# RWKV-7 scan on one core: the four chunk matrices of a tile of 96 tokens, whole 96x96 products against stacked 32x32 tiles

## What is computed

```python
# S_t = S_{t-1} diag(w_t) + (S_{t-1} a_t) b_t^T + v_t k_t^T ; y_t = S_t r_t
def step(s, inp):
    r_t, w_t, k_t, v_t, a_t, b_t = inp
    sa = jnp.einsum('bhvk,bhk->bhv', s, a_t)
    s = s * w_t[:, :, None, :] + sa[..., None] * b_t[:, :, None, :] \
        + v_t[..., None] * k_t[:, :, None, :]
    y_t = jnp.einsum('bhvk,bhk->bhv', s, r_t)
    return s, y_t
```

## Time and profile before

| | before |
|---|---|
| median of 3 runs | 2810.82 us (2810.22 to 2811.73) |
| profiled execution: its own time / its span | 2808.27 / 2806.5 us |
| PE, PEld, DVE, ACT busy | 94%, 92%, 64%, 42% of the span |
| granted TensorE clock, mean | 0.969 |
| scan loop | from about 1341 to 1854 us of the span |

### The profile page before, as it was taken

One profiled execution on the slowest core, in us unless ns is written; L12 is line 12 of the kernel. 1 busy time (PEld: TensorE's weight loads), 2 busy tenths in 40 slices (PEclk: granted clock), 3 DMA queues, 4 the chain that ended last, 5 costly groups with the idle time before them and its releaser, 6 DMA issues.

```text
span 2806.5 us, 54115 instructions
## 1 busy us (share of the span) xinstructions
PE 2639.1 (94%) x21933; PEld 2574.2 (92%) x21933; DVE 1782.8 (64%) x2235; ACT 1184.6 (42%) x1360; POOL 125.9 (4%) x121
## 2 busy tenths in 40 slices
PE   7999867999999999999899999989699999999996
PEld 7999857999999999999799999979699999999996
DVE  6675656666666666677656565556656666666666
ACT  4344523555444444456323222233444444444442
POOL 2000000100000000002000000000400000000003
PEclk9999978999999999999999999999799999999997
DMA  6555413565555556555232323334265555555552
GB/s 187 157 166 157 122 60 99 173 196 185 187 179 180 187 187 187 185 154 152 83 91 83 85 82 95 94 98 158 89 195 182 183 180 183 184 179 180 185 174 83
DMA packets 419321, 418.72 MB, mean 149 GB/s; under 512 B 15310, under 2 KB 417474, under 8 KB 418946
## 3 DMA queue, kind: packets, MB, share of 16 engines
q1 hardware_dynamic: 418722, 415.41, 48.2%
q10 hardware_dynamic: 496, 1.84, 0.2%
HBM read 415.10 MB, written 2.10 MB: 149 GB/s over the span
## 4 chain that ended last, share of the span: by engine, by line
PE 82%; DVE 10%; ACT 3%; PEld 2%; issue 1%; POOL 1%; DMA 0%; SPq 0%; ACTq 0%; DVEq 0%; POOLq 0%; PEldq 0%
PE psum L1887 25%; PE psum L1888 24%; PE psum L1889 24%; PE psum L2200 4%; DVE w_lo L998 3%; ACT w_hi L598 1%; DVE act_lo L1035 1%; DVE head_r L1109 1%; DVE mixed L1843 1%; PEld psum L1889 1%; PEld psum L1887 1%; PE psum L2356 1%; PEld psum L1888 1%; PE psum L2360 1%; PE psum L2251 1%
## 5 line engine op out<-in xcount | busy, mean ns | idle before, releaser
L1887 PE MATMUL psum<-act_hi,w_hi 128*128 128x256 f32 (+3 forms) x4880 | 1413.4, 290 | 54.2 <-DVE act_lo L1035 17.2
L1888 PE MATMUL psum<-act_lo,w_hi 128*128 128x256 f32 (+3 forms) x4880 | 1386.6, 284 | 0.0
L1889 PE MATMUL psum<-act_hi,w_lo 128*128 128x256 f32 (+3 forms) x4880 | 1383.0, 283 | 0.0
L598 ACT ACTIVATE w_hi<-raw 128x1024 fp32r<-128x1024 f32 x788 | 828.3, 1058 | 1138.0 <-PE psum L1889 1116.0
L998 DVE TENSOR_TENSOR w_lo<-raw,w_hi 128x1024 fp32r<-128x1024 f32 x788 | 958.2, 1229 | 503.2 <-ACT w_hi L598 502.3
L1887 PEld LDWEIGHTS psum<-act_hi,w_hi 128*128 128x128 f32 (+1 forms) x4880 | 928.4, 190 | 70.3 <-issue 28.9
L1888 PEld LDWEIGHTS psum<-act_lo,w_hi 128*128 128x128 f32 (+1 forms) x4880 | 929.2, 190 | 1.5 <-issue 0.7
L1889 PEld LDWEIGHTS psum<-act_hi,w_lo 128*128 128x128 f32 (+1 forms) x4880 | 928.8, 190 | 0.0
L1887 PE MATMUL psum<-ff_hi,w_hi 128*128 128x256 f32 x1280 | 363.7, 284 | 13.5 <-DVE up L1016 6.5
L1888 PE MATMUL psum<-ff_lo,w_hi 128*128 128x256 f32 x1280 | 361.4, 282 | 0.0
L1889 PE MATMUL psum<-ff_hi,w_lo 128*128 128x256 f32 x1280 | 361.2, 282 | 0.0
(11 more groups left out here) (338 smaller groups left out, 1811.5 us busy)
## 6 DMA issues: line engine op xcount, KB each, us to landing
raw<-in_w_in SPq DMA_DIRECT2D x188, 512.0 KB, 3.8
raw<-in_w_up SPq DMA_DIRECT2D x176, 512.0 KB, 3.6
raw<-in_w_down SPq DMA_DIRECT2D x176, 512.0 KB, 4.5
raw<-in_w_gate_up SPq DMA_DIRECT2D x176, 512.0 KB, 3.6
raw<-in_w_out SPq DMA_DIRECT2D x64, 512.0 KB, 4.5
x_rows<-in_x SPq DMA_DIRECT2D x2, 1024.0 KB, 6.2
out_x<-out_rows SPq DMA_DIRECT2D x8, 256.0 KB, 3.2
raw<-in_w_in SPq DMA_DIRECT2D x4, 384.0 KB, 3.4
```

Source lines behind the costliest of these rows:

```text
L598: act.activation(w_hi[:, slot], raw[:, slot], ACT.Copy).then_inc(S["hi_done"], 1)
L1887: pe.matmul(out_, wh, xh, start=first and r == 0, stop=False)
L1888: pe.matmul(out_, wh, xl, start=False, stop=False)
L1889: mm = pe.matmul(out_, wl, xh, start=False, stop=last and r == RK - 1)
```

## The change

Every product of the scan is cut to what is not known to be zero. Only the diagonal 32x32 chunk blocks of a score or power matrix are made; they stand stacked, chunk c on partitions 32c to 32c+31, 32 columns per head. So `ldt` to `p4` are [4, 32] instead of [4, 96] wide. Each product of a head becomes three, one per chunk, whose weights and results are at array position (32c, 32c); the scores are made at (64e, 32c), the parts of output and state at (32c, 64e) into three banks 5, 6, 7, one for each chunk, and the state steps at (64e, 64e) with a state of [128, 2, 64]. The masks are folded to 32 columns by POOL (11 more additions). The stages are merged into 12 slots with the same 336 rows; the last float32 stages before the steps are one stage, `um`. Some copies move between ACT and DVE. The zeroing of `mt` goes.

```diff
-            def each_head(lhs, rhs_, bank, wide=RB):
+            chunk = [slice(RC * c, RC * c + RC) for c in range(3)]
+            def each_tile(lhs, rhs_, bank, at, wide=RC):
                 for h in range(4):
-                    mm = pe.matmul(psum[0:RB, bank, wide * h:wide * h + wide], lhs[0:RB, h],
-                                   rhs_(h), start=True, stop=True)
+                    for s in chunk:
+                        mm = pe.matmul(psum[s, bank, at + wide * h:at + wide * h + wide],
+                                       lhs[s, h], rhs_(s, h), start=True, stop=True)
                 mm.then_inc(S["rw_tensor"], 1)
...
+                def scores(lhs, rhs, n, bank, at):
                     for p in range(2):
-                        for e in range(2):
-                            mm = pe.matmul(psum[0:RB, bank + e, 192 * p:192 * p + 192],
-                                           z_at(kind, e, p), a_and_r(e, p), start=True, stop=True)
+                        for c in range(3):
+                            for e in range(2):
+                                o = at + RC * n * p
+                                mm = pe.matmul(psum[chunk[c], bank + e, o:o + RC * n],
+                                               z_at(lhs, e, p, c), z_at(rhs, e, p, c, n),
+                                               start=True, stop=True)
...
+                scores(Z_B, Z_A, 2, 4, AT_LT)
+                scores(Z_A, Z_B, 1, 4, AT_L).then_inc(S["rw_tensor"], 1)
+                scores(Z_K, Z_A, 2, 6, 0).then_inc(S["rw_tensor"], 1)
                 fill()
                 pe.wait_ge(*rw_dve.at("rbt", it))
+                each_tile(M["ldt"], tile_of("ld"), 4, 0)
+                each_tile(M["ld"], tile_of("ldt"), 5, 0)
                 fill()
                 pe.wait_ge(*rw_dve.at("rkt", it))
...
+                pe.wait_ge(*rw_act.at("l2t_out", it))
+                pe.wait_ge(*rw_dve.at("l2_out", it))
+                each_tile(M["l2t"], tile_of("l2"), 5, 0)
+                each_tile(M["l2"], tile_of("l2t"), 4, 0)
+                each_tile(M["l2"], tile_of("p1"), 4, AT_P2)
                 fill()
                 pe.wait_ge(*rw_act.at("kv", it))
+                each_tile(M["akt"], lambda s, h: kv[s, 1, 64 * h:64 * h + 64], 7, 0, 64)
                 pe.wait_ge(*rw_act.at("l4_out", it))
                 pe.wait_ge(*rw_dve.at("p2", it))
+                each_tile(M["l4t"], tile_of("l4"), 5, 0)
+                each_tile(M["l4"], tile_of("p2"), 4, 0)
                 fill()
...
+                def by_head(lhs, rhs, at, wide, start=False, stop=False):
+                    for p in range(2):
+                        for c in range(3):
+                            for e in range(2):
+                                o = psum[halfp[e], STEP_BANK + c, at + wide * p:
+                                         at + wide * p + wide]
+                                mm = pe.matmul(o, lhs(chunk[c], 2 * p + e), rhs(chunk[c], 2 * p + e),
+                                               start=start and p == 0, stop=stop,
+                                               skip_group_check=True)
+                    return mm
+                by_head(u_part(0), tile_of("rbt"), AT_RU, RC, True, True)
+                by_head(u_part(0), b_part, AT_MT, 64, False, True)
+                by_head(u_part(1), tile_of("rbt"), AT_Y, RC)
+                by_head(tok(kv, 1), tile_of("rkt"), AT_Y, RC)
+                by_head(b_part, u_part(1), AT_ST, 64)
+                by_head(tok(kv, 0), tok(kv, 1), AT_ST, 64).then_inc(S["rw_tensor"], 1)
+                fill()
+                pe.wait_ge(*rw_dve.at("mt", it))
                 for c in range(3):
+                    pe.wait_ge(S["rw_s"], 10 * q + 1 + 3 * tt + c)
                     for p in range(2):
+                        for e in range(2):
+                            at = AT_Y + RC * p
+                            pe.matmul(psum[halfp[e], STEP_BANK + c, at:at + RC], st[halfp[e], p],
+                                      ru[halfp[e], p, RC * c:RC * c + RC], start=False, stop=True,
+                                      skip_group_check=True)
                     for p in range(2):
-                        mm = pe.matmul(psum[:, 4 + c, P * p:P * p + P], mt[:, c, p], st[:, p],
-                                       start=False, stop=True, skip_group_check=True)
+                        for e in range(2):
+                            at = AT_ST + 64 * p
+                            mm = pe.matmul(psum[halfp[e], STEP_BANK + c, at:at + 64],
+                                           mt[halfp[e], c, p], st[halfp[e], p], start=False,
+                                           stop=True, skip_group_check=True)
                     mm.then_inc(S["rw_tensor"], 1)
                     fill()
```

```diff
-    SLOTS = 17
+    SLOTS = 12
...
-            want = (2, 2, 2, 1, 2, 1, 1, 2, 2, 2, 2, 2, 2, 1, 1, 1, 2)[s] if it < 9 else \
-                (3, 2, 2, 2, 2, 2, 1, 2, 2, 2, 2, 2, 2, 2, 1, 1, 3)[s]
+            want += (2, 2, 2, 2, 3, 2, 2, 2, 3, 2, 2, 3)[s] if it < 9 else \
+                (3, 3, 3, 2, 3, 3, 2, 3, 3, 2, 2, 3)[s]
...
                     dve.wait_ge(*rw_pe.at(f"step{c}", it))
-                    for e in range(2):
-                        h = slice(64 * e, 64 * e + 64)
-                        src = psum[h, 4 + c, 0:256].rearrange("p (a k) -> p a k", a=2)[:, :, h]
-                        w = M["wc"][h, 2 * q:2 * q + 2, 3 * tt + c:3 * tt + c + 1]
-                        dve.tensor_tensor(st[h, :, h], src, w.to_broadcast([64, 2, 64]),
-                                          ALU.mult).then_inc(S["rw_s"], 1)
+                    w = M["wc"][:, 2 * q:2 * q + 2, 3 * tt + c:3 * tt + c + 1]
+                    dve.tensor_tensor(
+                        st[:], steps[:, c, AT_ST:AT_ST + 128].rearrange("k (p j) -> k p j", p=2),
+                        w.to_broadcast([P, 2, 64]), ALU.mult).then_inc(S["rw_s"], 1)
```

More of the change, by code:

```diff
@@ L300, in over, with four @@
         return wide.to_broadcast(shape)
[L302 to L304 removed]
+    def four(bank, at):
+        return psum[0:RB, bank, at:at + 4 * RC].rearrange("p (h t) -> p h t", t=RC)
+    AT_LT, AT_L, AT_P2 = 0, 128, 128
+    AT_RU, AT_MT, AT_ST, AT_Y = 0, 64, 192, 320
+    STEP_BANK = 5
     def unit_rows(w):
@@ L335, in rows_by_slot @@
                 ends.append(n)
-        assert len(ends) == len(LOOP_IN2)
+        assert at == 336 and len(ends) == len(LOOP_IN2)
         return table, ends
@@ L907, in _ @@
                 serve()
+                act.wait_ge(*rw_pe.at("l2t", it))
+                act.activation(M["l2t"][0:RB], four(5, 0), ACT.Copy).then_inc(S["rw_scalar"], 1)
                 serve()
@@ L937, in _ @@
                                psum[0:RB, 4, 0:512], ACT.Copy).then_inc(S["rw_scalar"], 1)
-                for _ in range(9, SLOTS):
+                for _ in range(5, SLOTS):
                     serve()
@@ L1594, in mask4, with masked @@
             def mask4(name):
-                m = M[name][0:RB]
+                m = M[name][0:RB, 0:RC]
                 return over(over(m, 1, 2), 1, 2)
-            def masked(dst, banks, at, wide, mask):
-                src = psum[0:RB, banks:banks + 2, 0:2 * wide] \
-                    .rearrange("s e (p w) -> s e p w", p=2)[:, :, :, at:at + RB]
+            def masked(dst, bank, at, mask, part=None):
+                src = psum[0:RB, bank:bank + 2, at:at + 64 if part is None else at + 128]
+                if part is None:
+                    src = src.rearrange("s e (p t) -> s e p t", p=2)
+                else:
+                    src = src.rearrange("s e (p a t) -> s e p a t", p=2, a=2)[:, :, :, part]
                 dve.tensor_tensor(heads4(dst), src, mask4(mask), ALU.mult) \
@@ L2309, in _ @@
                 fill()
                 pe.wait_ge(*rw_dve.at("z", it))
-                each_head(p4, lambda h: zz[0:RB, h], 6, P)
+                each_tile(M["p4"], tile_of("rhs"), 4, 0, P)
                 fill()
                 pe.wait_ge(*rw_dve.at("u", it))
-                for p in range(2):
-                    for e in range(2):
-                        h = 2 * p + e
-                        mm = pe.matmul(psum[halfp[e], 7, RB * p:RB * p + RB],
-                                       uu[0:RB, 0, h], M["rbt"][0:RB, h],
-                                       start=(p == 0), stop=True, skip_group_check=True)
```

213 lines of the change are left out of this document (80 added, 133 removed).

## The result

The changed kernel takes 2749.03 us (median of four runs, 2745.77 to 2754.38), the kernel before beside it 2810.68 us: ratio 0.9782, 95% interval 0.9765 to 0.9799. Forecast were 2738 us and a range of 2695 to 2815. The profiled execution took 2745.77 us, 62.5 less than that of before; the forecast for it was 2735.6.

The account below looks back on a forecast made before the run. PE's instruction queue bounds the scan: 14.5 us per iteration against 20.5, times 12, is 72 us, plus 0.7 for the dropped `memset`; 2808.3 - 72.7 = 2735.6, and 2.5 for the median gives 2738 us, range 2695 to 2815.

Parts of the forecast that it names:

- What bounds the kernel: Scan loop: it lasts as long as PE's instruction queue (PE busy 460.7 of 465.2 us), so PE's saving reaches the end.
- Positions side by side, priced at 0.87 ns times the larger width: Scan's float32 pairs (weight load plus matmul): cost follows the larger width, array positions overlap; 32-wide taken as 30 ns.
- Change of mode: Each of the 12 scan slots: entering and leaving small tiles costs some 0.34 us, 4.1 us per iteration.
- Scores and state parts: Scan stages over six positions: scores 0.57 us, the six `by_head` with 144 pairs 1.35 us per iteration, before mode changes.
- 0.95 us for hand-offs and instructions: Per scan iteration: chosen allowance for exposed hand-offs, DVE sometimes late, and PE's more than doubled instruction stream; at most 3 us.
- 14.5 us per iteration: PE's scan work after the change: 13.55 us of work and modes plus the allowance, against 20.5 us before.
- Rival 1, shared banks: `each_tile`: row groups sharing one PSUM bank take turns, three times its work, 48 us more than before, 2859; chance 0.12.
- Rival 2, a floor per matmul: Scan's 480 pairs not 128 wide: minimum time each; 18 ns gives 2775, 25 ns 2815, 38 ns 2890; chance 0.13.
- Rival 3: Scan's small tiles: array positions don't run side by side at all, 35.4 us per iteration, 2990; chance 0.02.
- Rival 4, hand-offs or clock: Loop: DVE's side work late in most slots, 2775; 1.2 GHz for a tenth of the loop besides, 2795; chance 0.08.
- Signs: Changed profile: y copies 396 to 402 us apart, PE busy 97%, DVE waits within 1 us per iteration, clock 1.00.
- main case: Whole kernel: narrow tiles overlap and the scan shortens as priced, 2738 us, own range 2705 to 2780; chance 0.65.

## Why the prediction was right, and where it was off

- **What bounds the kernel.** Right: the scan lasts as long as PE's queue, and each us saved in it arrived at the end; the work behind it kept its 953 us in these two profiles.
- **Positions side by side, priced at 0.87 ns times the larger width.** Right. The three 128-wide products were put at 1.22 us with their modes and cost 1.20; a narrow call was put at 0.24 and takes 0.26; the steps 0.79 and 0.81. The run with chunks outside shows that it is the innermost loop over positions that buys this, for which the earlier trace rows against the earlier trace rows had been the argument.
- **Change of mode.** Right: 0.34 forecast, 0.35 measured by adding 69 of them.
- **Scores and state parts.** Too cheap by 0.2 us each: 144 pairs of `by_head` take 1.54 us from first to last start (1.58 in the mean), 11 ns a pair, where 56 ns over six positions gave 9.4 and 1.35 us. Six positions don't quite give twice what three do: the 64-wide product over three takes 0.47 us for 24 pairs, 20 ns each.
- **0.95 us for hand-offs and instructions.** As a sum right (14.5 us per iteration in the table), but it was a choice. That the sum fits is in part luck: what filled it was the wait for ACT's copy of `l8` (5.0 us in the loop), issue gaps (3.1 us) and the two stages above, where hand-offs late by DVE and the instruction stream were meant.
- **The step that was wrong: nothing was put beside the 14.5, and the clock was taken to stay at 1.00.** The prediction named DVE's side work as "now and then" late within the slots, but not PE's own side matmuls that wait for it. With 12 slots per iteration instead of 17 a group of the projection ends every 7 slots instead of about 10, while the side work's distances from it, in slots, stay as they were; its steps on DVE and ACT then meet the scan's hand-offs. By the program DVE takes k's steps and then r's, and k's last part is held back to 8 slots after the end of k: for the first group that was slot 17, ahead of the end of r in slot 19, and is now slot 15, behind the end of r in slot 14, so that r's product comes later behind that end, while PE's sums of it stay 8 slots behind the end of r. The waits at L2187 cost 9.7 us, and the 17.0 us at half clock some 7 more. (414.2 - 234 - 5.5) / 11 is 15.9 us per iteration, 1.4 above the forecast: 15 us in the loop. 5 of them come back before the first copy of y, where 11.8 us were saved and 6.7 forecast, which is luck: without them the forecast would have been off by 15 and not by 10. Moving the side work later, and nothing else, took 21 us out of the loop.
- **Rival 1, shared banks**, is refuted: 24 pairs of 128 width of three row groups go into one bank and take 0.80 us, where taking turns would need 24 x 0.109 = 2.6 us. The rule in the Trainium skill ("TensorEngine Tiling (Array Packing)", Restrictions and Gotchas) that row tiles may not access a bank together does not show in this trace for tiles that write different partitions.
- **Rival 2, a floor per matmul**: no floor of that size per start; 10.7 ns is the spacing across three positions. The 25 ns of the Trainium skill ("TensorE: Matmul & The Clock Gate", Back-to-back issue gap) do not hold across positions. A limit of nearly the same size does exist in the supply of instructions, but it bites only in long narrow stretches, and cost 3 us here, if the packets are its cause. Rival 3 is refuted by the same rows.
- **Rival 4, hand-offs or clock**, is where the missing 10 us went, at about a quarter or a fifth of its price (37 to 57 us).
- **Signs.** The copies of y were to be 396 to 402 us apart and were 414.2; with the side work later, 392.9. PE's share of 97% came out at 96. The waits on DVE, within 1 us per iteration by forecast, are 10.1 us in eleven, so they kept to it, but three of 3.2 us make nearly all of them; with ACT's 5.0 and the issue gaps it is 1.7 per iteration. The clock, forecast at 1.00, was at 0.50 for 17.0 us. The range and the main case's own 2705 to 2780 held.

## What to carry to other kernels

Block-diagonal work on TensorE pays when it is issued round robin over the positions of the array and gathered in few stages: here a change of mode with its return costs 0.35 us, as much as 33 narrow pairs. When slots are merged, everything that is timed in slots has to be timed anew: three numbers of side work gave back a third of what the whole change had saved. And a wait of 3 us on PE can cost more than 3 us, since the clock often falls with it: with three such waits gone, the loop was 14.9 us shorter.

## What the runs showed of the hardware

- Three row groups side by side: 10.7 ns per 32-wide float32 pair, 35 ns per 128-wide one (0.80 us from the first to the last of 24 starts), all into one bank on different partitions. The same pairs with eight in a row for one position: 24 and 75 ns (0.55 and 1.72 us).
- Instructions reach PE in packets of 16 KB, some 256 instructions, never less than 3.3 us apart in the loop. Stretches of narrow pairs then stand still for up to 3.2 us at a time ("issue"): 3.1 us in the loop of the changed kernel, 18.1 with 192 pairs more per iteration, 7.2 when the same pairs are dealt out, none with the changed kernel's pairs dealt out. All 30 such gaps over 0.3 us in these traces end 2.2 to 3.0 us after the start of a packet. That the packets are the cause is argued from this, not tried by itself.
- PE idle for 3.2 us in the loop, with the clock at 1.00 before: it fell to 0.50 all nine times in the changed kernel and in those with the narrow products twice and with chunks outside, for 3.4 to 6.8 us (5.45 of 6.8 busy in the window shown). With 3.4 us idle it fell three times of three, for 10.2, 10.2 and 3.4 us. Behind the loop, waits of 3.1 and 3.2 us brought a fall in 15 cases of 20.
- After 17 waits of 1.3 to 2.0 us in the loops of all these kernels it fell five times, for 3.4 us, each within 0.5 to 1.3 us after the wait's end, and stayed at 1.00 twelve times; among six of 1.7 us for the same copy on ACT, it fell once.
- The changed kernel's runs lie 8.6 us apart, those of before 1.5: the mean granted clock goes with it, 0.966 in the shortest and 0.962 in the longest.
